# One channel tile of a depthwise convolution moved from TensorE's packed matmuls to GpSimd

## The reference, cut to what matters

```python
u = h @ w_in[i]
u_a, u_b = u[..., :c0], u[..., c0:c1]           # 512 channels each
u = u_a * jax.nn.sigmoid(u_b)
y = lax.conv_general_dilated(u, dw_w[:, None, :], window_strides=(1,),
    padding=[(CONV_WIDTH - 1, 0)], feature_group_count=D_CONV)   # 31 taps
y = y + dw_b
y = layernorm(y, ln_w, ln_b)
return jax.nn.silu(y)
```

## Time and profile before

| what | value |
|---|---|
| median of 3 runs | 914.06 us (913.45 to 914.6) |
| the profiled execution's own time | 913.59 us |
| its span | 911.7 us |
| busy: PE, PEld | 898.6 us (99%), 809.1 us (89%) |
| busy: DVE, ACT, POOL | 648.9 us (71%), 505.5 us (55%), 310.1 us (34%) |
| chain that ended last | PE 91%, DVE 4%, DMA 2%, ACT 2%, issue 1% |
| GpSimd's longest wait for ScalarE's `w_hi` | 226.6 us |

### The profile page before, as it was taken

The page is one execution under the profiler, slowest core; times in us unless marked ns, Lnnn a source line. Parts: engine busy times, 40 slices in busy tenths (PEclk is TensorE's granted clock), DMA queues, the critical chain, the costliest instruction groups (busy, mean ns, idle before and its releaser), DMA issues.

```text
span 911.7 us, 16491 instructions
## 1 busy us (share of the span) xinstructions
PE 898.6 (99%) x6900; PEld 809.1 (89%) x6900; DVE 648.9 (71%) x804; ACT 505.5 (55%) x747; POOL 310.1 (34%) x117
## 2 busy tenths in 40 slices
PE   8999999999999999999999999999999999999997
PEld 7998986888888878999999989998999888888886
DVE  5986747888883257758798765857655689999623
ACT  7534747455554446755656565555545566666532
POOL 4000001666665410000000005846685166666542
PEclk9999999999999999999999999999999999999999
DMA  9693464555555544555545435443455365555551
GB/s 358 224 277 120 155 226 147 200 190 188 188 193 212 185 167 166 185 175 185 186 141 186 157 95 189 140 144 135 142 206 185 119 237 192 191 193 194 187 190 47
DMA packets 32299, 164.01 MB, mean 180 GB/s; under 512 B 9154, under 2 KB 11602, under 8 KB 13794
## 3 DMA queue, kind: packets, MB, share of 16 engines
q1 hardware_dynamic: 32162, 162.89, 52.0%
q0 software_dynamic: 64, 0.08, 0.0%
HBM read 161.40 MB, written 1.57 MB: 179 GB/s over the span
## 4 chain that ended last, share of the span: by engine, by line
PE 91%; DVE 4%; DMA 2%; ACT 2%; issue 1%; SPq 0%; DVEq 0%; ACTq 0%
PE ring L1699 31%; PE acc L1829 18%; PE ring L1733 9%; PE acc L1733 8%; PE ring L1780 6%; PE ring L1737 5%; PE acc L1737 4%; DMA raw<-wstream 2%; DVE w_lo L1116 1%; PE acc L1881 1%; PE acc L2038 1%; PE acc L1842 1%; PE acc L2134 1%; PE ring L1805 1%; PE ring L1718 1%
## 5 line engine op out<-in xcount | busy, mean ns | idle before, releaser
L642 POOL TENSOR_TENSOR w_lo<-raw,w_hi 128x1024 fp32r<-128x1024 f32 x101 | 289.9, 2872 | 579.1 <-ACT w_hi L690 579.0
L690 ACT CAST w_hi<-raw 128x1024 fp32r<-128x1024 f32 x284 | 297.1, 1052 | 312.3 <-PE ring L1699 124.5
L1116 DVE TENSOR_TENSOR w_lo<-raw,w_hi 128x1024 fp32r<-128x1024 f32 x183 | 229.1, 1263 | 119.1 <-ACT w_hi L690 109.7
L1699 PE MATMUL ring<-h,w_hi 128*128 128x256 f32 x1344 | 246.1, 285 | 2.0 <-issue 1.2
L1699 PEld LDWEIGHTS ring<-h,w_hi 128*128 128x128 f32 x1344 | 209.6, 192 | 3.7 <-issue 3.2
L1699 PE MATMUL ring<-h,w_lo 128*128 128x256 f32 x672 | 190.1, 283 | 0.0
L1699 PEld LDWEIGHTS ring<-h,w_lo 128*128 128x128 f32 x672 | 128.8, 192 | 1.3 <-issue 1.3
L1829 PE MATMUL acc<-w_hi,ff 128*128 128x512 f32 x340 | 91.1, 390 | 0.0
L1733 PE MATMUL ring<-h,w_hi 128*128 128x512 f32 x352 | 88.1, 392 | 0.0
L1733 PE MATMUL acc<-h,w_hi 128*128 128x512 f32 x336 | 84.6, 394 | 0.0
L1829 PEld LDWEIGHTS acc<-w_hi,ff 128*128 128x128 f32 x340 | 63.6, 188 | 13.2 <-DVE w_lo L1116 0.2
(11 more groups left out here) (283 smaller groups left out, 1286.6 us busy)
## 6 DMA issues: line engine op xcount, KB each, us to landing
raw<-wstream SPq DMA_DIRECT2D x142, 1024.0 KB, 4.9
u<-uconv SPq DMA_DIRECT2D x4, 426.0 KB, 9.9
toep_t<-toep SPq DMA_DIRECT2D x16, 96.0 KB, 3.1
x<-x_tok SPq DMA_DIRECT2D x2, 512.0 KB, 4.6
mem<-mem_tok SPq DMA_DIRECT2D x1, 1024.0 KB, 11.2
w_ple<-wproj SPq DMA_DIRECT2D x1, 1024.0 KB, 7.2
out_t<-y SPq DMA_DIRECT2D x4, 256.0 KB, 2.2
decay<-decay_tab SPq DMA_DIRECT2D x1, 768.0 KB, 6.5
```

The lines of the kernel that those rows point to most:

```text
L642: nc.gpsimd.tensor_tensor(w_lo[:, u % UNITS], unit_of_raw(u), as_f32(w_hi[:, u % UNITS]), ALU.subtract).then_inc(lo_ready["pool"], 1)
L690: nc.scalar.copy(w_hi[:, u % UNITS], unit_of_raw(u)).then_inc(hi_ready, 1)
L1116: V.tensor_tensor(w_lo[:, u % UNITS], unit_of_raw(u), as_f32(w_hi[:, u % UNITS]), ALU.subtract).then_inc(lo_ready["dve"], 1)
L1699: last = mm(dst, w[a], src[:, b, kt], start=n == 0 and i == 0, stop=n == kts - 1 and i == 2)
```

## The change

Tile 1 of the convolution leaves TensorE and goes to GpSimd. `PACKED` has two tiles. GpSimd, after its `w_conv`, waits for tile 1 of `conv_in` and for each tap after the first issues a multiplication with the tap's weight into a scratch tile (`sq`, planes 6 and 7 in turn) and an addition of the scratch to `conv_y`; the first tap is a single multiplication with the bias added. TensorE waits for its signal, `pooled_out`, before the mean. Sizes that follow `PACKED` shrink with it: the round trip through DRAM, the packed weights, ScalarE's evictions.

```diff
-PACKED = (1, 2, 3)
+PACKED = (2, 3)
+POOLED = (1,)
...
+            pool.wait_ge(pad_ready, 2)
+            for j in POOLED:
+                wait_read(pool, "conv", j)
+                sums_at = {}
+                for w in range(CW):
+                    src, weight = conv_in[:, j, w:w + S], col("dw_w", w * 4 + j)
+                    if w == 0:
+                        added = link(nc.gpsimd.tensor_scalar(conv_y[:, j], src, weight, col("dw_b", j), ALU.mult, ALU.add))
+                        continue
+                    if w > 2:
+                        pool.wait_ge(pool_chain, sums_at[w - 2])
+                    scaled = link(nc.gpsimd.tensor_scalar(sq[:, 6 + w % 2], src, weight, None, ALU.mult))
+                    pool.wait_ge(pool_chain, scaled)
+                    ins = nc.gpsimd.tensor_tensor(conv_y[:, j], conv_y[:, j], sq[:, 6 + w % 2], ALU.add)
+                    if w < CW - 1:
+                        sums_at[w] = link(ins)
+                ins.then_inc(pooled_out, 1)
+
             feed(ahead_target(fi("mhg", 1)))
...
-            seen, tap_of = [0] * 4, [CW if t in PACKED else 0 for t in range(4)]
+            seen, tap_of = [0] * 4, [CW if t in PACKED + POOLED else 0 for t in range(4)]
...
             pe.wait_ge(packed_out, len(PACKED))
+            pe.wait_ge(pooled_out, len(POOLED))
             pe.wait_ge(conv_ready, 1)
```

More of the change, by code:

```diff
@@ L385, in program @@
         packed_out = sem("packed_out")
+        pooled_out = sem("pooled_out")
         rope_ready = sem("rope_ready")
```

## The result

The changed kernel takes 937.8 us (936.6 to 938.2, 4 runs) against 914.3 (913.5 to 915.2) on the same chip: 1.0257 of the time before, 95% interval 1.0244 to 1.0269, so 23.5 us slower. The direction was forecast, the size was not: 925 was said, within a range of 916 to 940. The profiled execution has a span of 935.5 us (911.7 before).

The account below looks back on a forecast made before the run. TensorE, busy 99% of the span, was taken as the bound. GpSimd's end at 28.4 + 34.1 + 30.8 = 93.3 against 82.6 adds 10.7 us to 913.6, 924.3; plus 0.5, 924.8, said as 925, range 916 to 940.

Parts of the forecast that it names:

- The mechanism: At the mean over the channels: TensorE waits for GpSimd, and all behind it is later by 10.7 us.
- The place of the wait: The mean's first matmul: released by `pooled_out`, with some 7 us of idle time on TensorE.
- GpSimd's own work: Tile 1's taps: 31 multiplications at 0.45 plus 30 additions at 0.67, 34.1 us (26.3 to 40.9).
- GpSimd's start: Tile 1 of `conv_in` written at 28.4 instead of 30.2, as VectorE keeps 1.8 us from the removed `w_conv`.
- at most it costs what an addition does: GpSimd's multiplication of 128x256: upper bound 0.67 us, the addition's price; 0.45 was taken from the selects.
- VectorE's turns: Beside GpSimd's taps: VectorE's instructions with two SBUF inputs put 30.8 us in 53 turns between GpSimd's.
- Scaling by columns: VectorE's turns: 1.0 us added to GpSimd's per 1024-column instruction, 0.5 for 512, 0.25 for 256.
- Their sum: GpSimd's end: 28.4 + 34.1 + 30.8 = 93.3 us, against 82.6, when the mean starts in the kernel before.
- TensorE's arrival: Before the mean: TensorE 7.2 us late at `v` 0, less 3.5 for the packed tile, stands there at 86.3.
- one-for-one turns: Shared port: while GpSimd has instructions left, each VectorE instruction with two SBUF inputs takes a turn.
- Rival B: GpSimd's taps: both instructions 0.67, 0.15 gap per addition, whole taps held; end at 110.9, 28 us late, 942; chance 0.17.
- Rival C: GpSimd's instructions fit VectorE's gaps, ending at 67; ending before 82.6 costs nothing; gain 4.3, 909.8 us; chance 0.08.

Follow-up runs that it names:

- the run with 112 matmuls: The changed kernel with 112 matmuls of the identity, results unused, on TensorE ahead of its wait for GpSimd; 940.0 us, ratio 1.0281.
- 18 taps: The changed kernel with GpSimd doing only taps 0 to 17 of tile 1, taps 18 to 30 left out; 911.6 us, ratio 0.9970.
- its removal alone: The kernel before with only GpSimd's third `w_conv` moved behind the gated input of tile 3; 912.8 us, ratio 0.9993.
- the run without taps: The changed kernel with VectorE doing 2 instead of 31 taps of tile 0, the other 29 left out; 935.1 us, ratio 1.0231.
- the tensor-tensor run: The changed kernel with GpSimd's 30 multiplications reading the weight as a second, repeated input in tensor-tensor form; 931.5 us, ratio 1.0185.
- four matmuls in that place: Kernel before with tile 1 split, 16 taps on GpSimd, rest on TensorE, plus four identity matmuls between the second and third transposes; 911.1 us, 0.9972.
- the kernel that this edit was made to: The kernel before with tile 1 shared: GpSimd taps 0 to 15, TensorE taps 16 to 30, VectorE adding the two; 912.9 us, ratio 0.9990.

## Why the prediction was wrong

The mechanism was right: GpSimd ends long after TensorE wants the tile, and all behind the mean is late by that. The place of the wait came out, and so did its releaser, which the run with 112 matmuls names; with 18 taps the loss is gone. The size did not come out, and it failed in one term above all, GpSimd's own work.

- GpSimd's start: 28.4 said, 29.2 measured; the 1.8 us of the `w_conv` came (its removal alone moved the gate from 29.76 to 27.96), the rest goes with a start of the program that is later (the first fill ends 1.9 us later). +0.8 us.
- GpSimd's own work: 34.1 us said, 52.2 measured (0.92 + 30 x 1.71). The multiplication was taken at 0.45 from the selects and bounded at 0.67 by the addition; it is 0.92, outside the bounds. That is the step that failed: "at most it costs what an addition does". One input was taken to be cheaper than two; on GpSimd the tensor-scalar form is the dearer one, by 0.20 over an addition and by 0.31 over the same multiplication in tensor-tensor form. Of the 18.1 us in all, 14.6 are the multiplications. The addition was near (0.67 for 0.72, 1.5 us), and 2.0 are the gap of 0.07 ahead of each addition, which the prediction took as filled by VectorE. The 14.6 alone are more than the whole error of 13.0.
- VectorE's turns: 30.8 us said, 76.5 - 52.2 = 24.3 measured. Scaling by columns made a tap 0.25 where the run without taps shows 0.09, which is 4.4 us of the difference. The rotation was taken at 8.0 and added 5.8 (four pairs from 67.06 to 79.70, less 1.71 each). Against that, two more `w_lo` and the transposed parts fell ahead of GpSimd's end, which the prediction had behind it. -6.5 us.
- Their sum: 93.3 + 0.8 + 18.1 - 6.5 = 105.7, the measured end. The two large terms err in opposite directions, so the total looks nearer than its parts.
- The clock behind a long idle time was left out: +1.6 us. The mean is 23.2 us late where 10.7 was said; with the 1.6 that makes 14.1 us too little, and the error is 13.0, because the idle gap of before in the second block is not in this trace.
- TensorE's arrival: 86.3 said, 80.2 measured. VectorE was held far less than one GpSimd instruction for each of its own, and no `w_lo` came late. The prediction's one-for-one turns are there with two-input instructions on GpSimd. That `v` 0 starts at 66.5 in the tensor-tensor run, for 66.6 said, is partly luck: GpSimd began there at 30.6, not at 28.4. This miss cost nothing, as the wait covers it.
- Rival B was nearest (942, above 932) for partly wrong reasons: both instructions at 0.67, 0.15 at each addition, and whole taps. The doubt that it was built on, a multiplication with a scalar that no row shows, was the right one.
- Rival C's threshold holds: with 18 taps the mean waits for nothing. Its gain is smaller than 4.3, by the later start and by `g` 0's wait.

Two statements of the Trainium skill meet these rows. It says that for GpSimd a "1-input is roughly line-rate" (GPSIMD Engine Reference, 4.1 Engine selection). Here the one-input form took 0.85 us without and 0.92 with a fetched scalar, the two-input forms 0.61 and 0.72, so for this size the measurement decides against it. No run here has another size, so what part of 0.85 goes by the column is not shown. And it says that the loser of the port "fully blocks" (SBUF — State Buffer, Who interferes with whom). For two-input instructions the tensor-tensor run agrees nearly: 1.60 us for 0.61 beside a subtraction, a hold of 0.99 of its 1.22, and 3.31 for 2.35 on the other side. For the multiplication with a fetched scalar it is lopsided: 2.95 for 0.92, and VectorE's two subtractions only 0.55 longer.

## What to carry to other kernels

Before a loop of small instructions goes to an idle engine, measure one of them there in the very form that the loop will have: a price taken from another operation was off by a factor of two, and 31 instructions carried it. Work it out as its own time plus what the neighbour's instructions put between, and compare with the moment of use; the idle engine has only that stretch, here 51 us, for 18 of 31 taps. And where a gain of 2 or 3 us is built from several edits, run the small ones alone, and look in the trace where the gain arises: here most of it arose 400 us behind the edits.

## What was not expected of the hardware

A GpSimd tensor-scalar multiplication of 128x256 took 0.92 us, the tensor-tensor one 0.61. The one with a scalar in SBUF was held by up to two VectorE instructions in a row (2.95 us), with a constant by one (1.90). Replacing the form with tensor-tensor speeds GpSimd up and slows VectorE down, from 2.90 to 3.31 us for a pair of subtractions.

TensorE's granted clock fell to 0.50 in the first fill of five kernels (the changed one among them), which had idle gaps of 0.3 to 1.2 us between the transposes. With four matmuls in that place it read 1.00, and the slow group of eight records took 1.21 us. But the kernel that this edit was made to also reads 1.00 there, with the slow group at 1.91, and so does the one with 112 matmuls. What makes that group slow, and whether the clock does, is not shown.

Left open: why the second half of x came at 7.5 to 8.4 us in the kernels with taps on GpSimd and at 7.2 to 7.7 in the four without, and what the idle gaps of 0.9 to 1.75 us without a releaser in the second block are.
